# Sums of squares taken with 128 columns of ones instead of one, the ranks' roots placed a slab later, and two banks of the forget values swapped

## What is computed

```python
def rms_norm(x, g):
    xf = x.astype(jnp.float32)
    y = xf * lax.rsqrt(jnp.mean(xf * xf, axis=-1, keepdims=True) + EPS)
    return (y * g.astype(jnp.float32)).astype(x.dtype)
...
        q = (rms_norm(c_q, q_norm[i]) @ w_uq[i]).reshape(B, S, MLA_HEADS, QK_HEAD_DIM)
        kv = (rms_norm(c_kv, kv_norm[i]) @ w_ukv[i]).reshape(B, S, MLA_HEADS, QK_NOPE_DIM + V_HEAD_DIM)
...
        hm = rms_norm(hm, mlstm_norm[i].reshape(MLSTM_HEADS, MLSTM_HEAD_DIM)).reshape(B, S, MLSTM_WIDTH)
...
        od = rmsnorm(od, subln_g) * (1.0 - lambda_init)
```

## Time and profile before

| | |
|---|---|
| median of 3 runs | 1373.33 us (1372.34 to 1375.85) |
| the profiled execution | 1370.14 us, of which the span from first to last instruction is 1368.4 us |
| PE busy | 1303.8 us, 95% of the span |
| weight loads (PEld) | 1099.3 us, 80% |
| DVE, ACT busy | 770.6 us (56%), 551.4 us (40%) |
| mean granted PE clock | 0.989 |

### The profile page before, as it was taken

One profiled execution on the slowest core, in us unless ns is written; L12 is line 12 of the kernel. 1 busy time (PEld: TensorE's weight loads), 2 busy tenths in 40 slices (PEclk: granted clock), 3 DMA queues, 4 the chain that ended last, 5 costly groups with the idle time before them and its releaser, 6 DMA issues.

```text
span 1368.4 us, 17737 instructions
## 1 busy us (share of the span) xinstructions
PE 1303.8 (95%) x6524; PEld 1099.3 (80%) x6524; DVE 770.6 (56%) x1235; ACT 551.4 (40%) x909; POOL 44.9 (3%) x47
## 2 busy tenths in 40 slices
PE   7999898999999999999999998999899999999996
PEld 6887687798888888888778887788798788888886
DVE  5866566465544544322684886677686622355334
ACT  5646555443323223322553654456443222232221
POOL 4000000000000000000030000000000000000002
PEclk9999999999999999999999999999999999999998
DMA  5222000411232223332223322321312223232322
GB/s 187 74 96 77 32 32 1 138 47 63 93 106 93 92 92 123 108 107 97 88 92 108 108 78 82 101 65 47 108 47 77 91 95 104 87 101 92 108 92 77
DMA packets 36957, 119.94 MB, mean 88 GB/s; under 512 B 4492, under 2 KB 6540, under 8 KB 36896
## 3 DMA queue, kind: packets, MB, share of 16 engines
q1 hardware_dynamic: 36320, 117.46, 26.2%
q0 software_dynamic: 576, 1.65, 0.4%
HBM read 111.74 MB, written 2.11 MB: 83 GB/s over the span
## 4 chain that ended last, share of the span: by engine, by line
PE 76%; DVE 14%; ACT 5%; issue 3%; DMA 1%; POOL 0%; POOLq 0%; ACTq 0%; SPq 0%; DVEq 0%
PE bank L819 24%; PE bank L821 23%; PE bank L820 23%; DVE w_lo L1945 3%; DVE tiles L1945 2%; DVE arena L1945 2%; DVE tiles L1948 1%; ACT w_hi L1404 1%; DMA raw_slab<-in_stream 1%; PE bank L970 1%; DVE negmax L2163 1%; DVE arena L1948 1%; DVE probsT L1945 1%; PE bank L916 1%; ACT arena L1425 1%
## 5 line engine op out<-in xcount | busy, mean ns | idle before, releaser
L1945 DVE TENSOR_TENSOR w_lo<-raw_slab,w_hi 128x1024 fp32r<-128x1024 f32 x198 | 243.7, 1231 | 287.8 <-ACT w_hi L1404 269.9
L819 PE MATMUL bank<-u_hi,w_hi 128*128 128x512 f32 x824 | 324.8, 394 | 6.5 <-DVE w_lo L1945 2.5
L821 PE MATMUL bank<-u_hi,w_lo 128*128 128x512 f32 x824 | 322.2, 391 | 0.0
L820 PE MATMUL bank<-u_lo,w_hi 128*128 128x512 f32 x824 | 322.0, 391 | 0.0
L819 PE MATMUL bank<-arena,w_hi 128*128 128x512 f32 (+1 forms) x692 | 262.8, 380 | 16.6 <-DVE w_lo L1945 7.6
L1404 ACT ACTIVATE w_hi<-raw_slab 128x1024 fp32r<-128x1024 f32 x188 | 198.0, 1053 | 179.8 <-PE bank L821 176.4
L820 PE MATMUL bank<-arena,w_hi 128*128 128x512 f32 (+1 forms) x692 | 259.5, 375 | 0.0
L821 PE MATMUL bank<-arena,w_lo 128*128 128x512 f32 (+1 forms) x692 | 259.5, 375 | 0.0
L819 PEld LDWEIGHTS bank<-u_hi,w_hi 128*128 128x128 f32 x824 | 155.4, 189 | 41.0 <-DVE w_lo L1945 3.5
L821 PEld LDWEIGHTS bank<-u_hi,w_lo 128*128 128x128 f32 x824 | 155.3, 188 | 33.0
L820 PEld LDWEIGHTS bank<-u_lo,w_hi 128*128 128x128 f32 x824 | 155.5, 189 | 30.6
(11 more groups left out here) (258 smaller groups left out, 1551.1 us busy)
## 6 DMA issues: line engine op xcount, KB each, us to landing
raw_slab<-in_stream SPq DMA_DIRECT2D x206, 512.0 KB, 3.4
arena<-arena SPq DMA_DIRECT2D x32, 128.0 KB, 2.3
residual<-in_xT SPq DMA_DIRECT2D x8, 256.0 KB, 7.5
out_hT<-residual SPq DMA_DIRECT2D x16, 128.0 KB, 1.7
arena<-forget_rows SPq DMA_DIRECT2D x8, 128.0 KB, 2.3
tiles<-in_pT POOLq DMA_DIRECT2D x2, 256.0 KB, 3.0
tiles<-bias_rows POOLq DMA_DIRECT2D x1, 512.0 KB, 4.0
early<-in_positions POOLq DMA_DIRECT2D x1, 256.0 KB, 3.4
```

The costliest lines, as they stand in the source:

```text
L819: pe.matmul(o, ws[0], xs[0], start=first, stop=False)
L820: pe.matmul(o, ws[0], xs[1], start=False, stop=False)
L821: return pe.matmul(o, ws[1], xs[0], start=False, stop=last)
L1945: return nc.vector.tensor_tensor(o, a, b, op)
```

## The change

It has three parts.

1. `stat` and `head_stats` go through a new function `summed`, which takes the column of ones broadcast to 128 columns as the moving operand. The result is 128 equal columns, written at columns `c` to `c + 127` of the bank. Only the first is wanted; the next token tile overwrites the other 127, and columns 0 to 15 end as before. The number of matmuls and their stationary operands stay.
2. The ranks' roots on ACT and their reciprocals on DVE come one slab later, behind the conversion of the slab for "mo0".
3. A new semaphore `ctx_read` counts the first of the two steps of `df_head`, and frees bank 5 in place of `ctx_scaled`. The values "fv2" and "fv3" swap banks: 3, 4, 6, 5 in place of 3, 4, 5, 6.

```diff
-                free = {"ml": (sem.sq_done, SQ0["ml"] + u // ST + 1), "df": (sem.ctx_scaled, u // ST + 1)}
+                free = {"ml": (sem.sq_done, SQ0["ml"] + u // ST + 1), "df": (sem.ctx_read, u // ST + 1)}
...
-        use(f"fv{t}", t + 3, slab("fv", 3), split(f"fv{t}"))
+        use(f"fv{t}", (3, 4, 6, 5)[t], slab("fv", 3), split(f"fv{t}"))
...
+            ones = col("one").to_broadcast([P, P])
+
+            def summed(o, c, square_, first, last):
+
+                return pe.matmul(o[:, c:c + P], square_, ones, start=first, stop=last)
+
             def stat(name):
...
-                            last = pe.matmul(o[:, i:i + 1], early[:, RANK_SQ[k], i * P:(i + 1) * P], col("one"), start=k == 0, stop=k == 1)
+                            last = summed(o, i, early[:, RANK_SQ[k], i * P:(i + 1) * P], k == 0, k == 1)
...
-                        last = pe.matmul(o[:, i:i + 1], square_[:, i * P:(i + 1) * P], col("one"), start=n == 0, stop=n == len(squares) - 1)
+                        last = summed(o, i, square_[:, i * P:(i + 1) * P], n == 0, n == len(squares) - 1)
...
-                        last = pe.matmul(o[:, h * ST + i:h * ST + i + 1], squares(h)[:, i * P:(i + 1) * P], col("one"), start=True, stop=True)
+                        last = summed(o, h * ST + i, squares(h)[:, i * P:(i + 1) * P], True, True)
...
             slab_hi(SLAB0[DENSE[0]])
-            root("cq", Q_RANK)
-            root("ckv", KV_RANK)
...
                     slab_hi(SLAB0[name] + 1)
+                if i == 0:
+                    root("cq", Q_RANK)
+                    root("ckv", KV_RANK)
...
             slab_lo(SLAB0[DENSE[0]])
-            inverse_root("cq")
-            inverse_root("ckv")
...
                 slab_lo(SLAB0[name] + 1)
+                if n == 0:
+                    inverse_root("cq")
+                    inverse_root("ckv")
...
-                    link(nc.vector.tensor_scalar(kept[:, h], o[:, :], DOWN, CLAMP, ALU.mult, ALU.min))
+                    nc.vector.tensor_scalar(kept[:, h], o[:, :], DOWN, CLAMP, ALU.mult, ALU.min).then_inc(sem.ctx_read, 1)
+                    dve.wait_ge(sem.ctx_read, h + 1)
                     nc.vector.tensor_scalar(kept[:, h], kept[:, h], -CLAMP, None, ALU.max).then_inc(sem.ctx_scaled, 1)
```

More of the change, by code:

```diff
@@ L553, in __init__ @@
         self.df_stat = new("df_stat")
+        self.ctx_read = new("ctx_read")
         self.sel_set = new("sel_set")
```

## The result

The changed kernel takes 1366.23 us (median of 4 runs, 1365.34 to 1367.93), beside 1374.59 (4 runs, 1372.34 to 1376.50) for the kernel before: 0.9946 of its time, interval 0.9925 to 0.9968. The four runs of before beside the first result lie high among the 84.

What follows compares the result with a forecast made beforehand. PE was taken as the bound, busy 95% of the span. Terms +0.2 - 1.6 - 0.1 - 0.9 + 0 = -2.4 us took the median 1373.3 to 1370.9 us, range 1367.5 to 1374.3.

Steps and rivals of the forecast that it cites:

- The reading: At long runs of one-column matmuls: PE counts as busy, but its clock falls to 0.50 right behind them.
- nothing happens: Rival: the clock follows waiting alone, so the falls stay despite wide sums; 1373.5 us, chance 0.08.
- The direct cost: At all widened sums: each group's last record comes 0.025 us later, about half on the path; +0.2 us.
- Ranks: At the ranks' sums: the fall from 67.3 to 70.7 goes, where PE is the bound behind it; -1.6 us.
- Roots later: At the ranks' roots, moved a slab later: the delay is covered by DVE's wait for PE; 0 us.
- Banks: At "fv2" and "fv3": PE gets 1.25 us ahead but gives it back waiting before the differential heads' sums; 0 us.
- a dear broadcast: Slower rival, at every sum: the broadcast moving operand takes 0.23 us a record, not 0.117; 1389 us, chance 0.05.
- the mLSTM heads' -0.9: At the mLSTM heads' spreads: the fall from 214.1 may move into PE's longer wait for the factors; bounds 0 and -1.6.
- What a fall costs: Wherever PE is the bound: a fall of 3.4 us slows 8 matmuls by 0.20 us each, losing 1.6 us.
- the 0 for the differential heads: At their sums: the fall behind goes, but the longer wait ahead likely draws another; 0 us, -1.6 as other end.
- the level: Starting time: the profiled execution's difference was moved to the median of three, 1373.3 us.
- all three keep the clock: Rival: all three long runs, the differential heads' too, keep the clock; -4.0 us, 1369.3 us, chance 0.25.

Runs made afterwards that it cites:

- the 84: All runs of the kernel before, unaltered, over three batches of the follow-up experiments: mean 1371.2 us.
- wide_ranks: The kernel before with only the ranks' 24 sum records widened to 128 columns of ones: mean 1368.9 us, ratio 0.9989.
- wide_heads: The kernel before with only the mLSTM heads' and differential heads' 64 sum records widened to 128 columns: mean 1367.7 us, ratio 0.9982.
- wide_later: The kernel before with wide sums and the differential heads' sums behind the third eighth of the values; old banks, old roots: mean 1365.6 us, ratio 0.9961.
- roots_only: The kernel before with only the ranks' roots and reciprocals a slab later: mean 1372.0 us, ratio 1.0001.
- banks_only: The kernel before with only ctx_read and the values' banks 3, 4, 6, 5: mean 1373.4 us, ratio 1.001.
- wide_only: The kernel before with only the sums widened to 128 columns of ones, roots and banks as before: mean 1365.8 us over 20 runs.
- after_again: The changed kernel measured again, unaltered: ratio 0.998 to before; mean 1367.5 us over 23 runs, a later repeat included.
- the 27: All runs of the changed kernel, the first result's four and 23 later ones: mean 1367.3 us.

## Why the prediction was wrong

The time between the same two conversions to `w_lo` on DVE gives each place its own price, over the 14 profiles. The numbers are us, each the mean of as many profiles as stand beside it (those of the kernels with moved sums left out of the last row):

| stretch of before | sums narrow | wide, old banks | wide, swapped banks | forecast |
|---|---|---|---|---|
| ranks, 64.9 to 121.8 | 57.3 (4) | 55.3 (10, all banks) | | -1.6 |
| mLSTM, 194.6 to 263.6 | 69.5 (4) | 68.5 (10, all banks) | | -1.0 |
| differential heads, 843.4 to 877.6 | 35.1 (4) | 32.8 (4) | 33.8 (3) | 0 |

**What held.** *The reading*, that a narrow matmul keeps PE busy and not its clock, is shown by `wide_ranks` and `wide_heads`, where width is all that was changed at each place. The Trainium skill ("TensorE: Matmul & The Clock Gate", table "Why this matters for your kernels") ties falls to idle gaps between bursts of matmuls. The stretch at 201.0 of `wide_ranks`, right behind 3.7 us of unbroken narrow work (197.20 to 200.90), doesn't agree with that as the only cause. The rival built on it, nothing happens, is out. One slip of the reading: the prediction counts the fall at 214.1 among those of the attention passes, but it stands at the mLSTM heads' spreads, as its own later section has it. *The direct cost* was right: 0.1 us for a run of 32, and a record 23 ns longer. *Ranks:* the clock stays and DVE goes on 1.66 us earlier, as the sum had it. *Roots later:* nothing. *Banks:* PE's waits moved as worked out (0.76 and 2.51 for 0.9 and 2.8), and the sums start 6.97 us behind DVE's first step before and after, so no sooner against the chain. The clock fell on the longer wait in two of the three profiles of the changed kernel. The slower rival, a dear broadcast, is out.

**Right in number by luck: the mLSTM heads' -0.9.** The wait for the factors grew to 2.07 us (2.3 forecast). But the fall that was to come in this wait and be over by 214 did so in one profile of ten, `wide_later`: it starts at 206.1, right at the wait's end, and the second head's spread takes 1.15 us. In the other nine it starts 1.4 to 2 us behind the end of the wait (at 207.7 in the changed kernel), lasts 6.8 or 10 us, and that spread still takes 2.08 us (at 211.59). From the conversion at 194.6 to that at 244.4, `wide_later` takes 48.3 us, the profile that I had read 49.8, the other nine 49.8 to 51.3. The place gains on the mean only because the other three profiles with narrow sums have a longer fall, from 211 or 215 on, and take 51.4: 51.0 narrow against 50.3 wide, 0.7 us. The row of the table has 1.0, with a wait for `w_lo` in it that is up to 1.6 us long in 5 of the 14 profiles, narrow or wide.

**The first step that failed is "What a fall costs": 3.4 us a fall, 1.6 us lost.** I read all falls from one execution, where each but the last lasts 3.4 us. In two of the four profiles with narrow sums (`roots_only`, `banks_only`) the fall behind the ranks' sums lasts 6.8 us and the stretch takes 57.7 us, not 56.9; in two (`banks_only`, `wide_ranks`) that behind the differential heads does, 35.9 us, not 34.2. The mean loss is 2.0 at the ranks and 2.3 at the differential heads, not 1.6. At the ranks that is 0.4 of the 1.5 us by which the sum fell short of the -3.9 measured. The profiled execution had its seven falls of 3.4 us, 24 us, and by its mean clock some 30 us with the one at its end; the 84 average 37 us at half clock. Their times follow that number with a correlation of 0.92, 0.42 us for each us at half clock, from 1365.4 to 1377.7 us in all. `wide_only` has 21 us: 16 us less by 0.42 is 6.7, where 5.4 were measured.

**The second, and the largest in the sum, is the 0 for the differential heads together with the 0 for the banks.** The widening alone is worth 2.3 us at this place, not the 1.6 of the other end, and the swap takes about 1 of them back (33.8 against 32.8), by the runs 1.5 (0.4 to 2.6). I had seen the mechanism and priced the two at once, so that the swap looked free. It is not. Where the clock falls under the wide sums the stretch takes 34.3 us, as in the profile of before (34.2), which is the 0 of the sum; that is so in two of the three profiles. In the third (`after_again`) the clock holds through the same wait and it takes 32.7, as in `wide_only`. `banks_only` holds it through that wait too, so "more often than not" rests on two of four. And before itself takes 35.1 on the mean, not 34.2, so what is left is 1.3 us and not 0. With the sizes measured, -2.0 - 0.7 - 1.3 = -4.0, beside -3.9 in the runs.

**The third is the level.** The median of three that I started from, 1373.3, is 2.1 us above the mean of the 84, and the profiled execution 1.1 below it. Moving the difference of one execution to a median of three put 2 us too much on the forecast. A sum of -3.9 from 1371.2 ends at 1367.3, just below the range. What of the first result's -8.4 goes beyond -3.9 is luck of its few runs: the four of before lie 3.4 us above the mean of the 84, the four of the changed kernel 1.1 below that of the 27. The rival "all three keep the clock", -4.0 us and 1369.3, came nearest in size, but describes `wide_only` (-5.4 measured) and not the changed kernel.

What stays open: what makes a fall last 3.4, 6.8 or 10 us, why the clock falls on the wait of 2.5 us in some executions and not in others, and why the falls in the attention passes come and go.

## What to carry to other kernels

Where PE is the bound, look for short falls of the clock at 1 us, and behind long runs of matmuls with one moving column first. Here they counted as busy and were followed by half speed, and widening them to 128 columns cost 0.1 us for 32 records. Before moving a stall, find the wait that it lengthens and what will run behind it; here a freed bank paid only together with work put into that wait. And when the loss is in something that varies between executions, take its size from many executions, with the mean clock of each as the gauge, and no single profile as the typical one.

## What the hardware showed unexpectedly

Falls of the clock lasted 3.4, 6.8 or 10 us: 6.8 us at 64.5, 719.9 and 856.4 in `banks_only`, 10 us at 207.8 in the changed kernel. A float32 matmul with a new stationary operand takes its 0.12 us a record with 1 moving column and with 128, and 32 records take 5.5 us in place of 3.9 where the clock is at half for 3.2 us of them. The same kernel on one core varies by 12 us of 1371 before and by 8 of 1367 after, and the time goes with that at half clock (correlation 0.92 before, 0.72 after).
